# FFN up projections: wide and narrow matmuls taken in turn instead of in runs of 16

## The chip, the cores and the metric

The kernel runs on one core of a Trainium2 chip. The metric is the device time of one execution in microseconds, the median of three runs. TensorE does the matmuls, VectorE and ScalarE the arithmetic around them, GpSimd (POOL) some small things, and SyncE (SP) issues the loads of weights.

## What is computed

A decoder trunk of four layers on 256 tokens of width 1024, in float32. Each layer is half an FFN, a mixer, and half an FFN again, each on a normalised input and added to the residual. The change touches the FFNs alone, of which there are eight:

```python
def swiglu(x, wi, wo):
    gate, up = jnp.split(x @ wi, 2, axis=-1)
    return (jax.nn.silu(gate) * up) @ wo
# for each layer i
h = h + 0.5 * swiglu(rmsnorm(h, ln_ffn1[i]), ffn1_wi[i], ffn1_wo[i])
h = h + mix
h = h + 0.5 * swiglu(rmsnorm(h, ln_ffn2[i]), ffn2_wi[i], ffn2_wo[i])
```

wi has 1024 rows and 2 x 2816 columns, wo has 2816 rows and 1024 columns.

## The kernel before

Float32 products are made of float32r passes. Each operand is split into a high part (rounded) and a low part (the rest), and a product is high x high + high x low + low x high. `whi` and `wlo` hold the two parts of a piece of weights, in a ring of 3 slots; `xT` holds the transposed activations, for each of 8 blocks of 128 rows the high part (256 tokens) and right behind it the low part (256 tokens); `xT_hi` and `xT_lo` are views of it.

The up projection is made transposed: the weights are the stationary operand and the tokens move. So one wide matmul (line 699, `up_both`) with a block of `whi` and all 512 columns of `xT` makes high x high in the left half of a PSUM bank and weight-high x token-low in the right half. One narrow matmul (line 707, `up_rest`) with a block of `wlo` and the 256 columns of `xT_hi` adds the third product to the left half. `psum[:, 4 + blk, :]`, blk 0 to 3, are the four banks: 0 and 1 hold 256 gate columns, 2 and 3 the 256 up columns of a chunk. In the trace an operation is written out<-moving,stationary: `psum<-xT,whi` is the wide and `psum<-xT,wlo` the narrow one.

An FFN has 11 chunks of 256 hidden columns (`FC`). Each takes three pieces of weights: A (rows 0 to 511 of wi, part 0), B (rows 512 to 1023, part 1), C (256 rows of wo, of the chunk before). A part is 4 banks x 4 row blocks k, that is 16 wide and 16 narrow matmuls. Before the change part 0 does its 16 wide ones, then its 16 narrow ones; part 1 the 16 narrow ones, then the 16 wide ones, and after the wide ones of blk 1 it increments `proj_done`, on which ScalarE's gate copy (line 762) waits. The last matmul of each part increments `piece_used`, on which the conversion of the piece after next on ScalarE (lines 474, 478), the up copy (line 766) and by way of them the loads wait. Then come 24 wide matmuls of the down projection (line 536). The waits ahead of blk 0 and 2 of part 0 (`proj_read`) are for the sums on VectorE (lines 815, 821) that read those banks for the chunk before. The order of each engine's work is written out by hand, chunk by chunk; eight chunks of an FFN run in a hardware loop.

The first part 0 of each FFN is in `first_piece`, woven with the transposes of the normalised input. In chunk 0 the matmul of the row scales (line 868) stands after blk 1 of part 1, as `between`.

ScalarE makes `whi` from the loaded `raw`, VectorE then makes `wlo` (line 497). `wlo` of an up piece is not laid out as `whi`: it is moved by `SHIFT` and each row block by a further `STEP`.

```python
SHIFT, STEP = 16, 32
```

Block (k, blk) of `whi` begins at word k x 512 + blk x 128 of its slot, the same block of `wlo` at 16 + k x 544 + blk x 128. Block k of `xT` begins at word k x 512. The `wlo` of other pieces has no shift. The mixer's line 994 (`turned_half`) makes projections with 256 moving columns, weights of `whi` and `wlo` in turn, both without a shift, and moving tokens from `xT`.

Of the kernel before, what the change touches and what calls it, by code (L numbers as in the profile page):

```python
# [27 lines left out]
P = 128  # L28
SEQ = 256
# [8 lines left out]
FC = 256  # L38
CHUNKS = D_FF // FC
RING = 3  # L40
PCOLS = 2048
SHIFT, STEP = 16, 32
# [94 lines left out]
def trunk(nc, x, positions, ln_ffn1, ffn1_wi, ffn1_wo, ln_mix, ln_ffn2, ffn2_wi, ffn2_wo,  # L137
# [3 lines left out]
    with ctx:  # L141
        def sb(name, shape, dt=F32):
            return ctx.enter_context(nc.sbuf_tensor(name, shape, dt))
# [6 lines left out]
        whi = sb("whi", [P, RING, PCOLS], F32R)  # L150
        wlo = sb("wlo", [P, RING, PCOLS + P], F32R)
        h = sb("h", [P, TT, D])
        xT = sb("xT", [P, KD, 2, SEQ], F32R)
        xT_hi, xT_lo = xT[:, :, 0, :], xT[:, :, 1, :]
# [28 lines left out]
        psum = ctx.enter_context(nc.psum_tensor("psum", [P, 8, NCOL], F32))  # L183
# [363 lines left out]
        def out_group(pe, slot, g, xh, xl, k0, first, last):  # L547

            t, nh = GROUPS[g]
            for k in range(2):  # L550
                m = passes(pe, psum[:, g, :], xh[:, k0 + k, t * P:(t + 1) * P], xl[:, k0 + k, t * P:(t + 1) * P],
                           slot, slice(k * D + nh * NCOL, k * D + (nh + 1) * NCOL), first and k == 0, last and k == 1)
            return m
# [27 lines left out]
        def norm_fill0(j):  # L581
            return 0 if j == 0 else subs[j - 1].norm_fill0
# [64 lines left out]
        def first_piece(pe, j):  # L647
# [9 lines left out]
            if s.kind != "ffn" and s.kind != "ml":  # L657
                pe.wait_ge(tr_read, q + 2)
                m = turned_half(pe, s, 0, 0, 0)
                norm_fill(pe, j, 3)  # L660
                m = turned_half(pe, s, 0, 0, 1)
            elif s.kind == "ffn":
                pe.wait_ge(tr_read, q + 2)
                up_both(pe, slot, 0, 0, None if j else lambda k: first_wait(pe, k))
                if j:
                    norm_fill(pe, j, 3)
                up_both(pe, slot, 0, 1)
                up_both(pe, slot, 0, 2)
                up_both(pe, slot, 0, 3)
                for blk in range(4):  # L670
                    m = up_rest(pe, slot, 0, blk)
            else:
                for t in range(TT):
                    if t:
                        norm_fill(pe, j, 3)
                    pe.wait_ge(tr_read, q + t + 1)
                    m = project(pe, slot, t, UP[0][t], 0, p.tiles, p.cols, True, False)
            m.then_inc(piece_used, 1)

        def last_piece(pe, s, n, xh, xl, k0):  # L680

            j = s.index + 1
            pe.wait_ge(lo_ready, n + 1)
            for g in range(4):
                m = out_group(pe, n % RING, g, xh, xl, k0, False, True)
                m.then_inc(acc_done if g < 3 else piece_used, 1)
                if g == 2 and j < len(subs):
                    norm_fill(pe, j, 0)
                    norm_fill(pe, j, 1)
            if j < len(subs):  # L690
                first_piece(pe, j)


        def up_both(pe, slot, part, blk, ready=None):

            for k in range(4):
                if ready:
                    ready(k)
                i = pe.matmul(psum[:, 4 + blk, :], whi[:, slot, k * 2 * FC + blk * P:k * 2 * FC + (blk + 1) * P],  # L699
                              xT[:, 4 * part + k, :, :].rearrange("p a n -> p (a n)"),  # L700
                              start=part == 0 and k == 0, stop=part == 1 and k == 3, skip_group_check=True)
            return i

        def up_rest(pe, slot, part, blk):

            for k in range(4):
                i = pe.matmul(psum[:, 4 + blk, 0:SEQ], wlo[:, slot, SHIFT + k * (2 * FC + STEP) + blk * P:SHIFT + k * (2 * FC + STEP) + (blk + 1) * P],  # L707
                              xT_hi[:, 4 * part + k, :], start=False, stop=False, skip_group_check=True)
            return i

        def ffn_pe(pe, s):
            n0, b0, c0 = s.piece0, s.block0, CHUNKS * s.ffn

            def up(m, c, part, between=None):
                pe.wait_ge(lo_ready, m + 3 * c + 1)
                if part == 0:
                    for blk in range(4):
                        if blk % 2 == 0:
                            pe.wait_ge(proj_read, 2 * b0 - 1 + blk // 2 + 2 * c)
                        up_both(pe, m % RING, 0, blk)  # L720
                    for blk in range(4):
                        i = up_rest(pe, m % RING, 0, blk)
                else:
                    for blk in range(4):
                        up_rest(pe, m % RING, 1, blk)
                    for blk in range(4):
                        i = up_both(pe, m % RING, 1, blk)
                        if blk == 1:
                            i.then_inc(proj_done, 1)
                            if between:  # L730
                                between()
                i.then_inc(piece_used, 1)

            def chunk(c):
                up(n0 - 1, c, 0)
                up(n0, c, 1)
                m = n0 + 1
                pe.wait_ge(lo_ready, m + 3 * c + 1)
                pe.wait_ge(hid_lo_done, c0 + c)
                for g in range(4):  # L740
                    i = out_group(pe, m % RING, g, hidT_hi, hidT_lo, 0, isinstance(c, int) and c == 1, False)
                i.then_inc(piece_used, 1)

            pe.wait_ge(tr_read, norm_fill0(s.index) + 4)
            up(n0 + 1, 0, 1, lambda: rows_pe(pe, s, 0))
            chunk(1)
            with pe.Fori(2, CHUNKS - 1) as c:
                chunk(c)
            chunk(CHUNKS - 1)
            pe.wait_ge(hid_lo_done, c0 + CHUNKS)  # L750
            last_piece(pe, s, n0 + 3 * CHUNKS - 1, xT_hi, xT_lo, 6)
# [114 lines left out]
        def rows_pe(pe, s, bank):  # L866
            pe.wait_ge(diag_done, s.rows0 + 1)
            pe.matmul(psum[:, bank, 0:SEQ], ones[:, :], diag[:, :, :].rearrange("p t n -> p (t n)"), start=True,
                      stop=True).then_inc(rows_done, 1)
# [1388 lines left out]
```

## Time and profile before

| | |
|---|---|
| median of 3 runs | 1925.06 us (1924.36 to 1925.41) |
| the profiled execution | 1924.97 us, span 1923.2 us |
| TensorE busy | 1901.9 us of the span, 99% |
| TensorE, weight loads | 1640.8 us, 85% |
| VectorE | 1366.2 us, 71% |
| ScalarE | 1128.9 us, 59% |
| DMA | 344.41 MB, mean 179 GB/s |

The span is the time from the first to the last instruction in the profile of one execution. Busy time of TensorE includes the modelled ends of the matmuls, which overlap the next ones; so the distance between two starts says more than a duration. A weight load has a row of its own (PEld) and runs beside the matmul ahead of it. "Idle before" is the time for which an engine sat idle ahead of an instruction, and after the arrow stands what released it.

### The profile page before, as it was taken

How to read it: one execution, taken by the hardware profiler on the slowest of the kernel's cores; microseconds unless marked ns; L12 is line 12 of the kernel's file. 1: busy time of each engine (PE TensorE's matmuls, PEld its weight loads, DVE VectorE, ACT ScalarE, POOL GpSimd, SP SyncE). 2: the span in 40 equal slices, each digit the busy share in tenths (PEclk: the TensorE clock that was granted, in tenths of full speed). 3: DMA queues.
4: the chain of work that ended last, by engine and by line, in shares of the span. 5: the costliest groups of instructions: out<-in, count | busy, mean ns of one | idle time of the engine just before them, and what ended most of it. 6: DMA issues, size and time to landing. Idle time of an engine off the chain costs nothing.

```text
span 1923.2 us, 29477 instructions
## 1 busy us (share of the span) xinstructions
PE 1901.9 (99%) x10740; PEld 1640.8 (85%) x10740; DVE 1366.2 (71%) x1844; ACT 1128.9 (59%) x1678; POOL 70.0 (4%) x151
## 2 busy tenths in 40 slices
PE   8999999999999999999999999999999999999998
PEld 6888988888888888888888889888888888978887
DVE  6766775777776687776776676676677777667666
ACT  6555575555655567655565555665555556656553
POOL 2000000000000002000010001000000000000000
PEclk9999999999999999999999999999999999999999
DMA  6555534655555554555655544355556555535553
GB/s 220 197 195 198 175 127 137 218 193 187 167 196 195 177 190 161 170 194 190 211 175 196 196 158 131 126 178 193 196 178 212 191 188 172 175 124 167 191 196 120
DMA packets 245263, 344.41 MB, mean 179 GB/s; under 512 B 12213, under 2 KB 197194, under 8 KB 245194
## 3 DMA queue, kind: packets, MB, share of 16 engines
q1 hardware_dynamic: 242016, 340.29, 53.6%
q10 hardware_dynamic: 3178, 3.18, 0.6%
q8 instruction: 46, 0.75, 0.2%
q14 instruction: 23, 0.19, 0.0%
HBM read 341.32 MB, written 1.06 MB: 178 GB/s over the span
## 4 chain that ended last, share of the span: by engine, by line
PE 93%; DVE 4%; ACT 2%; issue 0%; ACTq 0%; POOL 0%; POOLq 0%; DVEq 0%
PE psum L699 34%; PE psum L536 32%; PE psum L707 17%; PE psum L994 5%; DVE wlo L497 1%; PE psum L567 1%; PE psum L1645 1%; PE psum L1036 1%; DVE mix L1460 1%; ACT whi L478 1%; PE psum L1702 0%; DVE mix L1185 0%; PE psum L1047 0%; PE psum L1732 0%; PE psum L1609 0%
## 5 line engine op out<-in xcount | busy, mean ns | idle before, releaser
L478 ACT ACTIVATE whi<-raw,gains 128x512 fp32r<-128x512 f32 (+2 forms) x876 | 557.0, 709 | 255.1 <-PE psum L707 187.4
L699 PE MATMUL psum<-xT,whi 128*128 128x512 f32 x2816 | 679.2, 392 | 3.0 <-DVE wlo L518 2.5
L497 DVE SCALAR_TENSOR_TENSOR wlo<-raw,gains,whi 128x512 fp32r<-128x512 f32 (+2 forms) x876 | 596.1, 742 | 55.7 <-ACT whi L478 55.7
L699 PEld LDWEIGHTS psum<-xT,whi 128*128 128x128 f32 x2816 | 522.3, 188 | 111.9 <-issue 3.6
L707 PEld LDWEIGHTS psum<-xT,wlo 128*128 128x128 f32 x2816 | 333.2, 188 | 6.8
L707 PE MATMUL psum<-xT,wlo 128*128 128x256 f32 x2816 | 334.7, 276 | 0.0
L815 DVE TENSOR_TENSOR gate_in_T<-psum,low 128x512 f32<-128x512 f32 x88 | 60.9, 692 | 326.0 <-ACT low L762 326.0
L493 DVE TENSOR_TENSOR wlo<-raw,whi 128x2048 fp32r<-128x2048 f32 x100 | 228.6, 2286 | 42.8 <-ACT whi L474 42.8
L536 PE MATMUL psum<-whi,hidT_hi 128*128 128x512 f32 x640 | 249.0, 389 | 0.0
L536 PE MATMUL psum<-wlo,hidT_hi 128*128 128x512 f32 x640 | 249.0, 389 | 0.0
L536 PE MATMUL psum<-whi,hidT_lo 128*128 128x512 f32 x640 | 249.0, 389 | 0.0
L536 PE MATMUL psum<-whi,xT 128*128 128x512 f32 x704 | 229.8, 396 | 2.3 <-DVE xT L562 1.4
L474 ACT ACTIVATE whi<-raw 128x2048 fp32r<-128x2048 f32 x100 | 190.7, 1907 | 26.6 <-PE psum L707 24.5
L536 PEld LDWEIGHTS psum<-whi,xT 128*128 128x128 f32 x704 | 132.2, 188 | 32.7 <-DVE xT L562 3.0
L536 PEld LDWEIGHTS psum<-whi,hidT_hi 128*128 128x128 f32 x640 | 120.1, 188 | 25.0
L536 PEld LDWEIGHTS psum<-wlo,hidT_hi 128*128 128x128 f32 x640 | 120.1, 188 | 24.9
L536 PEld LDWEIGHTS psum<-whi,hidT_lo 128*128 128x128 f32 x640 | 120.1, 188 | 24.9
L536 PE MATMUL psum<-wlo,xT 128*128 128x512 f32 x352 | 137.2, 390 | 0.0
L777 ACT ACTIVATE hidT_hi<-hid 128x512 fp32r<-128x512 f32 x80 | 50.6, 633 | 142.7 <-PE psum L536 106.5
L770 ACT ACTIVATE silu<-gate_in_T 128x512 f32<-128x512 f32 x88 | 55.7, 634 | 106.9 <-DVE gate_in_T L817 106.8
L994 PE MATMUL psum<-xT,whi 128*128 128x256 f32 x576 | 107.1, 285 | 1.1 <-DVE mix L1170 1.1
L762 ACT ACTIVATE low<-psum 128x512 f32<-128x512 f32 x88 | 52.4, 596 | 82.4 <-PE psum L699 82.4
(224 smaller groups left out, 1527.6 us busy)
## 6 DMA issues: line engine op xcount, KB each, us to landing
raw<-in_ffn_wi SPq DMA_DIRECT2D x350, 512.0 KB, 4.6
raw<-in_ffn_wo SPq DMA_DIRECT2D x176, 512.0 KB, 4.4
raw<-in_sb_w_in SPq DMA_DIRECT2D x48, 512.0 KB, 4.6
raw<-in_ml_w_in SPq DMA_DIRECT2D x24, 512.0 KB, 4.6
raw<-in_sb_w_out SPq DMA_DIRECT2D x16, 512.0 KB, 4.0
raw<-in_ml_w_out SPq DMA_DIRECT2D x8, 512.0 KB, 4.0
raw<-in_mla_w_out SPq DMA_DIRECT2D x8, 512.0 KB, 4.2
raw<-in_mla_w_in SPq DMA_DIRECT2D x4, 512.0 KB, 4.2
```

The lines of the kernel that those rows point to most:

```text
L474: act.activation(whi[:, slot, 0:w], raw[:, slot, 0:w], ACT.Copy).then_inc(hi_ready, 1)
L478: last = act.activation(whi[:, slot, r], raw[:, slot, r], ACT.Copy, scale=gain_col(p.gain + k))
L493: dve.tensor_tensor(wlo[:, slot, p.at:p.at + w], raw[:, slot, 0:w], hi[:, 0:w], ALU.subtract).then_inc(lo_ready, 1)
L497: last = dve.scalar_tensor_tensor(wlo[:, slot, p.at + k * p.step + r.start:p.at + k * p.step + r.stop], raw[:, slot, r], gain_col(p.gain + ...
L536: m = pe.matmul(dst, a, b[:, slot, cols], start=first and n == 0, stop=last and n == 2)
L699: i = pe.matmul(psum[:, 4 + blk, :], whi[:, slot, k * 2 * FC + blk * P:k * 2 * FC + (blk + 1) * P], xT[:, 4 * part + k, :, :].rearrange("p ...
L707: i = pe.matmul(psum[:, 4 + blk, 0:SEQ], wlo[:, slot, SHIFT + k * (2 * FC + STEP) + blk * P:SHIFT + k * (2 * FC + STEP) + (blk + 1) * P], ...
L762: act.activation(low[:, 0, :, :], psum[:, 4:6, SEQ:2 * SEQ], ACT.Copy).then_inc(low_done, 1)
L770: act.activation(silu[:, :, :], gate_in_T[:, :, :], ACT.Silu).then_inc(silu_done, 1)
L777: act.activation(hidT(last)[0], hid[:, :, :], ACT.Copy).then_inc(hid_hi_done, 1)
L815: dve.tensor_tensor(gate_in_T[:, :, :], psum[:, 4:6, 0:SEQ], low[:, 0, :, :], ALU.add).then_inc(proj_read, 1)
L994: i = pe.matmul(dst, w[:, m % RING, c:c + P], v[:, k0 + k, :], start=k0 + k == 0 and a == 0 and blk == 0, stop=k0 + k == KD - 1 and a == 2 ...
```

## The change

The two matmuls get functions of their own, `up_wide` and `up_narrow`, and a new `up_mixed` takes them in turn: for each k, in part 0 wide then narrow, in part 1 narrow then wide. `ffn_pe` uses it in both parts. The matmuls, their operands, the waits and the increments are the same; `first_piece` keeps its order. In part 1 `proj_done` is incremented by the last wide matmul of blk 1, as before, which now has 8 narrow and 8 wide ones ahead of and with it instead of 16 narrow and 8 wide.

```diff
+        def up_wide(pe, slot, part, blk, k):
+
+            return pe.matmul(psum[:, 4 + blk, :], whi[:, slot, k * 2 * FC + blk * P:k * 2 * FC + (blk + 1) * P],
+                             xT[:, 4 * part + k, :, :].rearrange("p a n -> p (a n)"),
+                             start=part == 0 and k == 0, stop=part == 1 and k == 3, skip_group_check=True)
+
+        def up_narrow(pe, slot, part, blk, k):
+
+            c = SHIFT + k * (2 * FC + STEP) + blk * P
+            return pe.matmul(psum[:, 4 + blk, 0:SEQ], wlo[:, slot, c:c + P], xT_hi[:, 4 * part + k, :], start=False, stop=False,
+                             skip_group_check=True)
+
...
+        def up_mixed(pe, slot, part, blk):
+
+            for k in range(4):
+                if part == 0:
+                    up_wide(pe, slot, part, blk, k)
+                i = up_narrow(pe, slot, part, blk, k)
+                if part:
+                    i = up_wide(pe, slot, part, blk, k)
             return i
...
                     for blk in range(4):
                         if blk % 2 == 0:
                             pe.wait_ge(proj_read, 2 * b0 - 1 + blk // 2 + 2 * c)
-                        up_both(pe, m % RING, 0, blk)
-                    for blk in range(4):
-                        i = up_rest(pe, m % RING, 0, blk)
+                        i = up_mixed(pe, m % RING, 0, blk)
                 else:
                     for blk in range(4):
-                        up_rest(pe, m % RING, 1, blk)
-                    for blk in range(4):
-                        i = up_both(pe, m % RING, 1, blk)
+                        i = up_mixed(pe, m % RING, 1, blk)
                         if blk == 1:
                             i.then_inc(proj_done, 1)
```

## Rows read from the trace of the kernel before

**Rows 1.** The page: busy time, granted clock, and the chain by line.

```profile
PE 1901.9 (99%) x10740; PEld 1640.8 (85%) x10740; DVE 1366.2 (71%) x1844; ACT 1128.9 (59%) x1678; POOL 70.0 (4%) x151
...
PEclk9999999999999999999999999999999999999999
...
PE psum L699 34%; PE psum L536 32%; PE psum L707 17%; PE psum L994 5%; DVE wlo L497 1%; PE psum L567 1%; PE psum L1645 1%; PE psum L1036 1%; DVE mix L1460 1%; ACT whi L478 1%; PE psum L1702 0%; DVE mix L1185 0%; PE psum L1047 0%; PE psum L1732 0%; PE psum L1609 0%
```

**Rows 2.** Waits of TensorE over the whole span: total us, times, longest.

```profile
PE psum L2219 <- DMA mix<-in_ln_ffn: 6.0, 1, 6.0
PE psum L699 <- DVE wlo L518: 2.5, 2, 1.4
...
PE psum L699 <- DVE gate_in_T L815: 0.4, 1, 0.4
```

**Rows 3.** Timeline of TensorE in one FFN chunk: start us, us, what, count.

```profile
93.10 3.79 PE L699 MATMUL psum<-xT,whi 128*128 128x512 f32 x16
96.73 3.80 PE L707 MATMUL psum<-xT,wlo 128*128 128x256 f32 x32
100.36 3.81 PE L699 MATMUL psum<-xT,whi 128*128 128x512 f32 x16
104.02 0.39 PE L536 MATMUL psum<-whi,hidT_hi 128*128 128x512 f32 x1
```

**Rows 4.** Lines 699, 707: duration ns min/median/max; whole span, then from 100.36 on.

```profile
L699 PE MATMUL psum<-xT,whi x2816: 387/389/795, 10.5 to 1904.0; 128*128 128x512 f32 x188
...
L707 PE MATMUL psum<-xT,wlo x2816: 276/276/388, 19.2 to 1900.5; 128*128 128x256 f32 x188
...
L699 PE MATMUL psum<-xT,whi x1: 395/395/395, 100.4 to 100.4; 128*128 128x512 f32 x1
...
L699 PE MATMUL psum<-xT,whi x2: 395/396/397, 100.4 to 100.6; 128*128 128x512 f32 x2
...
L699 PE MATMUL psum<-xT,whi x2: 389/392/395, 100.8 to 101.1; 128*128 128x512 f32 x2
...
L699 PE MATMUL psum<-xT,whi x8: 389/389/393, 101.3 to 102.9; 128*128 128x512 f32 x8
...
L707 PE MATMUL psum<-xT,wlo x2: 276/277/278, 100.1 to 100.2; 128*128 128x256 f32 x2
```

**Rows 5.** The same: line 707 from 96.73 on, line 699's last before.

```profile
L707 PE MATMUL psum<-xT,wlo x3: 277/279/279, 96.7 to 97.0; 128*128 128x256 f32 x3
...
L707 PE MATMUL psum<-xT,wlo x20: 276/276/276, 97.8 to 99.9; 128*128 128x256 f32 x20
...
L699 PE MATMUL psum<-xT,whi x1: 388/388/388, 96.5 to 96.5; 128*128 128x512 f32 x1
```

**Rows 6.** Lines 994 and 1645, also 256 columns: durations, and part of the timeline.

```profile
L994 PEld LDWEIGHTS psum<-xT,whi x576: 186/192/192, 198.1 to 1672.5; 128*128 128x128 f32 x192
L994 PE MATMUL psum<-xT,whi x576: 278/283/467, 198.1 to 1672.6; 128*128 128x256 f32 x192
...
L1645 PE MATMUL psum<-sp_hi,whi x64: 276/280/416, 1170.0 to 1212.4; 128*128 128x256 f32 x64
...
198.70 0.28 PE L994 MATMUL psum<-xT,wlo 128*128 128x256 f32 x1
...
199.06 0.28 PE L994 MATMUL psum<-xT,wlo 128*128 128x256 f32 x1
```

**Rows 7.** Timeline of ScalarE and VectorE in the chunk of rows 3.

```profile
102.40 0.60 ACT L762 ACTIVATE low<-psum 128x512 f32<-128x512 f32 x1 [1.03 <-PE psum L699]
...
104.37 2.73 DVE L497 SCALAR_TENSOR_TENSOR wlo<-raw,gains,whi 128x512 fp32r<-128x512 f32 x4
```

**Rows 8.** Timeline at the first chunk: the diag tile on POOL, the row matmul.

```profile
19.71 1.21 POOL L2144 TENSOR_SCALAR diag<-ident,rstd 128x128 f32<-128x128 f32 x2
...
25.16 0.59 PE L868 MATMUL psum<-diag,ones 128*128 128x256 f32 x2
```

More of the change, by code:

```diff
@@ L698, in up_both @@
                     ready(k)
-                i = pe.matmul(psum[:, 4 + blk, :], whi[:, slot, k * 2 * FC + blk * P:k * 2 * FC + (blk + 1) * P],
-                              xT[:, 4 * part + k, :, :].rearrange("p a n -> p (a n)"),
-                              start=part == 0 and k == 0, stop=part == 1 and k == 3, skip_group_check=True)
+                i = up_wide(pe, slot, part, blk, k)
             return i
@@ L706, in up_rest @@
             for k in range(4):
-                i = pe.matmul(psum[:, 4 + blk, 0:SEQ], wlo[:, slot, SHIFT + k * (2 * FC + STEP) + blk * P:SHIFT + k * (2 * FC + STEP) + (blk + 1) * P],
-                              xT_hi[:, 4 * part + k, :], start=False, stop=False, skip_group_check=True)
+                i = up_narrow(pe, slot, part, blk, k)
+            return i
+        def up_mixed(pe, slot, part, blk):
+            for k in range(4):
+                if part == 0:
+                    up_wide(pe, slot, part, blk, k)
+                i = up_narrow(pe, slot, part, blk, k)
+                if part:
+                    i = up_wide(pe, slot, part, blk, k)
             return i
```

## The prediction

> **What bounds the kernel now.** I read the page first: TensorE is busy 99% of the span, and the chain that ended last lies for 34% on the wide up matmuls (line 699), 17% on the narrow ones (line 707) and 32% on the down projections and outputs (line 536) [rows 1]. TensorE's granted clock is in the top tenth in all 40 slices, so at the upper level of 2.4 GHz [rows 1]. Then the waits of TensorE: seven kinds, the longest 6.0 us in all, once, before the first matmul; the others are 2.5 us or less, down to 0.4 [rows 2]. So there is next to no wait to remove; the time is the number of matmuls times the distance from one start to the next, which I call the pitch. The timeline of one FFN chunk gives the pitches, by the difference of the starts of two groups divided by the count [rows 3]: 16 wide ones from 93.10 to 96.73, 3.63/16 = 0.227 us; 32 narrow ones (16 of each part) to 100.36, 3.63/32 = 0.1134 us; 16 wide ones to 104.02, 3.66/16 = 0.2288 us. Both widths cost the same 0.443 ns per column, with the weight load of each matmul hidden behind the matmul ahead of it. The third stretch is the same work as the first and takes 0.03 us longer. It is the one that follows narrow matmuls, and this is the row on which the forecast turns.
>
> The duration in a row is modelled and longer than the pitch, but it moves with it: 389 ns stands for a pitch of 227 and 276 for 113.4 [rows 3, 4], and 283 for 120 [rows 6], each 162 to 163 more. So differences of durations can be used as differences of pitch.
>
> **The change part by part.** Nothing is added or taken away: the same 2816 wide and 2816 narrow matmuls [rows 4], with the same operands, waits and increments. The first piece of each of the 8 FFNs keeps its old order (16 of each). That leaves 2816 - 8 x 16 = 2688 pairs whose order becomes wide, narrow, wide, narrow (in part 1 narrow first).
>
> Part A, the cost of a switch of width. Of a wide matmul after a narrow one the trace has an example in every chunk, 88 in all. The rows around 100.36 us show the first five wide durations as 395, 397, 389, 395, 393 and then 389 on and on [rows 4]: in the second row 397 is the new one beside 395, in the third 389 and 395, in the fourth 393 is the largest. The excess is 6 + 8 + 0 + 6 + 4 = 24 ns, which is the 0.03 us seen above. I read it as two regular reads (the moving columns and the next weights) that settle into a phase, and that a change of width unsettles. Of a narrow one after a wide one: 279, 279, 277, then 276 [rows 5], an excess of 3 + 3 + 1 = 7 ns, 80 of which would go (the 8 first pieces keep theirs). After the change every matmul of the 2688 pairs is the first after a switch, and none gets to settle. For the wide one I take +6, the value of a first one; its bounds are 387 - 389 = -2, the least wide duration at this line, and 397 - 389 = +8 [rows 4]. Sum: 2688 x 6 ns = 16.1 us.
>
> Part B, the narrow one. By its place it is a first one, +3. But what is loaded behind it changes too. Today the weights loaded during a narrow matmul are nearly always narrow ones (wlo, laid out at SHIFT and STEP, 16 + k x 544 + blk x 128 words); after the change they are wide ones (whi, at k x 512 + blk x 128, no shift). Line 994 is the nearest row with that: matmuls of the same width and type, with weights of whi and wlo both unshifted, and there the duration is 283, the weight load lasts 192 instead of 188, and three matmuls take 0.36 us, a pitch of 120 instead of 113.4 [rows 6]. That is +7. The one narrow matmul of a chunk that today loads whi behind it showed 278, +2 [rows 4], and line 1645, of the same width with whi as weights but another moving tile, has 276 at least and 280 as its median [rows 6], so the 7 isn't certain. Bounds: 0 (the 276) and +7. I take +5, midway between 3 and 7. Sum: 2688 x 5 = 13.4 us.
>
> The opposite of this could be true of the wide one: it would now load the shifted wlo behind it. The one wide matmul of a chunk that does so today lasted 388, against 389 [rows 5], so I count nothing for it, and keep it as a rival.
>
> Part C, what is removed. The switches of today vanish into the pairs: 88 x 24 ns + 80 x 7 ns = 2.1 + 0.6 = 2.7 us.
>
> The Trainium skill speaks of this on the page "TensorE: Matmul & The Clock Gate", section "What happens when you issue a matmul": weights and moving data have read ports of their own, so loading the next weights takes nothing from the running matmul. By that rule a pair costs the same in any order, and the result would be no change beyond part C, which is the time of the first rival below. The row of line 994 speaks against it: equal width, equal type, another address of the weights, and 6.6 ns more.
>
> Part D, the waits. The increment on the wide matmul of blk 1 in part 1 comes earlier: today after 16 narrow and 8 wide, then after 8 pairs, (16 x 113.4 + 8 x 227) - 8 x 340.4 = 0.9 us earlier. ScalarE sits in that wait for the gate copy (1.03 us ahead of 102.40), then VectorE waits for ScalarE; the copy, the gate sum and the conversion queued behind it on VectorE move 0.9 us ahead [rows 7]. That buys nothing: the conversion from 104.37 to 107.10 is wanted by TensorE after the 24 matmuls that start at 104.02 [rows 3], at 104.02 + 24 x 0.2267 = 109.46, so it is early already by 2.4 us. In part 0 the wait ahead of blk 2, for the up sum, is reached after 8 pairs in place of 8 wide ones, 0.9 us later: more slack; that ahead of blk 0 stays. At most the 0.4 us wait for the gate sum [rows 2] goes. The up copy still waits for the last matmul of part 1, whose place is the same. The increments on which the conversions and so the loads hang are on the last matmul of each part, as now, and no DMA or queue is moved. The small matmul of the row scales (line 868) comes 0.9 us earlier in the first chunk; its input is the diag tile, done at 19.71 + 1.21 = 20.92 with the matmul at 25.16, so of 4.2 us of cover 3.3 remain [rows 8]. I count D at zero. If that cover were gone, each us by which a conversion came too late would be a us more; it has 2.4 in hand, and a slower part gives it more.
>
> Sum: 16.1 + 13.4 - 2.7 = +26.8 us. The profiled execution took 1924.97 us, 0.1 below the median of 1925.06, with a span of 1923.2. Forecast: 1924.97 + 26.8 = 1951.8 us, +1.4%. By the bounds of this case, 6 + 3 = 9 and 8 + 7 = 15 ns per pair, 1946.5 to 1962.6.
>
> **The rivals.** First: the alternation settles into a phase of its own. Runs of one width do that within five matmuls, and a strict alternation is regular too. A settled pair costs 340 ns, nothing but part C is left, and the time is 1922.3. For it: how sharply both runs lock. Against: the narrow run and the wide run clearly don't share a phase, or the switch would cost nothing. With -2 on the wide one it would be 1916.9.
>
> Second, faster: the shifted layout helps whatever matmul it is loaded behind. It saves the narrow ones 120 - 113.4 = 6.6 ns; if wide ones gain as much once wlo is loaded behind them, and narrow ones keep their 113.4 with whi behind them (as the 278 half suggests), a pair falls by 6.6 and the time is 1924.97 - 17.7 - 2.7 = 1904.6. It decides if wide durations come out near 382. Against: the 388 of the one that does it today, and that nothing wide at line 699 lies below 387.
>
> Third, much slower: each pair pays the whole of both disturbances, 24 + 7 = 31 ns. That gives 2688 x 31 = 83.3, and 2005.6. Against: most of the 24 falls on later matmuls, which the next switch cuts off.
>
> **How the numbers follow.** Forecast 0.62. Settled alternation 0.15, of which 0.13 within 0.2% and 0.02 at its fast end. The layout gain 0.12. The whole price 0.06. A tax of a few ns per pair, between 1929 and 1946, 0.05. A measurement of this kernel can tell about 0.2%, 3.9 us. So slower 0.62 + 0.06 + 0.05 = 0.73, same 0.13, faster 0.14. The range from 1917 to 1963 takes in the forecast, the settled case and the small tax, 0.82; the forecast's own is 1946.5 to 1962.6.
>
> **What would show it.** In the profile after: the median of line 699 near 395 and of line 707 near 281; a chunk's up part of 16 pairs at 5.6 us instead of 5.44; line 536 still 389; the waits of TensorE no longer than now; line 762 starting 0.9 us earlier in its part. Medians of 389 and 276 mean the first rival, 382 the second. The forecast is wrong if the unsettled state isn't what a switch costs but what a long run of the other width leaves behind: then a single narrow matmul would disturb nothing.

## The result and the profile after

| | median | runs |
|---|---|---|
| before | 1924.71 us | 4 (1924.24 to 1925.41) |
| changed | 1950.22 us | 4 (1948.98 to 1951.53) |
| ratio | 1.0131 | 95% interval 1.0115 to 1.0147 |

The change costs 25.5 us, 1.3%. The forecast was 1951.8 us. The profiled execution took 1951.53 us with a span of 1949.8 us, 26.6 more than the 1923.2 of before.

The page of the changed kernel first: busy time of the engines, the chain by line, and the groups of the wide (now line 696) and the narrow matmul (now line 703), with busy us and mean ns.

```profile
PE 1927.1 (99%) x10732; PEld 1655.2 (85%) x10740; DVE 1371.6 (70%) x1844; ACT 1135.5 (58%) x1678; POOL 70.0 (4%) x151
...
PE psum L696 34%; PE psum L536 31%; PE psum L703 17%; PE psum L1009 5%; DVE wlo L497 2%; PE psum L1660 1%; PE psum L567 1%; ACT whi L478 1%; PE psum L1051 1%; DVE mix L1475 1%; PE psum L1717 0%; DVE mix L1200 0%; DMA raw<-in_ffn_wi 0%; DMA raw<-in_ml_w_in 0%; PE psum L1062 0%
...
L696 PE MATMUL psum<-xT,whi 128*128 128x512 f32 x2816 | 987.1, 397 | 1.5 <-DVE wlo L518 1.5
L703 PE MATMUL psum<-xT,wlo 128*128 128x256 f32 x2816 | 756.9, 281 | 0.0
```

The two groups invite a mistake. Together their busy time is 1744 us, while that of the same groups before, on the same page, was 1013.9 (679.2 and 334.7). That is not what the change costs: the busy time of a group merges its own matmuls where their modelled ends overlap. In a run a wide matmul adds its pitch of 227 ns to that sum. In alternation the next wide one starts some 351 ns later, so it adds 351, the narrow one's share included, and a narrow one adds its whole 281. TensorE as a whole went from 1901.9 to 1927.1, 25.2 us; the other 1.4 us of the span are time in which it sat idle. The means are of more use: 397 and 281.

The timeline of one chunk, with the start of each matmul in us:

```profile
77.53 0.39 PE L696 MATMUL psum<-xT,whi 128*128 128x512 f32 x1
77.75 0.28 PE L703 MATMUL psum<-xT,wlo 128*128 128x256 f32 x1
77.87 0.40 PE L696 MATMUL psum<-xT,whi 128*128 128x512 f32 x1
78.11 0.28 PE L703 MATMUL psum<-xT,wlo 128*128 128x256 f32 x1
78.22 0.39 PE L696 MATMUL psum<-xT,whi 128*128 128x512 f32 x1
78.45 0.28 PE L703 MATMUL psum<-xT,wlo 128*128 128x256 f32 x1
78.57 0.40 PE L696 MATMUL psum<-xT,whi 128*128 128x512 f32 x1
78.81 0.28 PE L703 MATMUL psum<-xT,wlo 128*128 128x256 f32 x1
78.92 0.39 PE L696 MATMUL psum<-xT,whi 128*128 128x512 f32 x1
...
88.77 0.39 PE L536 MATMUL psum<-whi,hidT_hi 128*128 128x512 f32 x1
```

This answers [rows 3]. From the first up matmul to the first down matmul it is 88.77 - 77.53 = 11.24 us, against 104.02 - 93.10 = 10.92 before; at the trace's ns it is 11240 and 10913, the same to 1 ns in each of the 72 chunks that stand between two down projections. The pattern repeats after two pairs: from 77.87 to 78.57 and from 78.22 to 78.92 are 0.70 us, so 350 ns a pair. The wide pitches are 229.3 and 235.9 in turn, the narrow ones 117.2 and 117.6. Part 1 takes five pairs to settle and is then in another cycle, with wide pitches of 235 to 236 and narrow ones of 117 to 118, 353 ns a pair, though wide and narrow take turns there with the same places of their weights. By part the chunk costs 5598 ns (5446 before) and 5642 ns (5467 before).

Durations of the two lines and of a down group (ns, min/median/max), against [rows 4]:

```profile
L696 PE MATMUL psum<-xT,whi x2816: 387/397/796, 10.9 to 1930.6; 128*128 128x512 f32 x188
...
L703 PE MATMUL psum<-xT,wlo x2816: 276/281/468, 19.2 to 1930.5; 128*128 128x256 f32 x188
...
L536 PE MATMUL psum<-whi,hidT_hi x640: 389/389/389, 38.7 to 1935.6; 128*128 128x512 f32 x160
```

The wide median went from 389 to 397, the narrow one from 276 to 281; the down projections stayed at 389. 327 ns x 72 steady chunks are 23.5 us of the 26.6. Part 1 of the first chunk and the whole second chunk of each FFN are in the new order too, but together they add only 1.1 us over the eight FFNs, because something is won there. The gate sum on VectorE that the second chunk's first matmul waits for, in one FFN before and after:

```profile
324.53 0.69 DVE L815 TENSOR_TENSOR gate_in_T<-psum,low 128x512 f32<-128x512 f32 x1 [2.69 <-ACT low L762]
...
326.77 0.69 DVE L830 TENSOR_TENSOR gate_in_T<-psum,low 128x512 f32<-128x512 f32 x1 [1.84 <-ACT low L777]
```

Before, the sum ends at 325.22, and the matmul that waits for it starts at 325.37, 396 ns behind the one ahead of it instead of 227; the next one is late by another 78. That is a stop of 0.25 us in seven FFNs and of 0.61 in one, 2.3 us in all. After the change the increment of `proj_done` comes earlier, the sum ends at 327.46, the matmul starts at 328.42, and no such distance is left. The remaining 2.0 us lie between the FFNs' chunks. 1.6 of them are one wait in a mixer (line 1645, now 1660), 0.8 us before and 2.4 after; it doesn't go with the order, since it is 0.8 in e2, which alternates too, and 2.4 in e7, which has runs.

The gate copy in the chunk of the timeline and the waits of TensorE:

```profile
86.15 0.60 ACT L777 ACTIVATE low<-psum 128x512 f32<-128x512 f32 x1 [0.19 <-PE psum L696]
```

```profile
PE psum L2234 <- DMA mix<-in_ln_ffn: 5.1, 1, 5.1
PE psum L1660 <- DVE mix L1946: 2.4, 1, 2.4
PE psum L696 <- DVE wlo L518: 1.5, 2, 1.1
PE psum L536 <- DVE xT L562: 1.4, 3, 0.6
```

The copy starts 86.15 - 83.13 = 3.02 us into part 1, against 102.40 - 98.55 = 3.85 before, so 0.83 us earlier. TensorE's waits came to 13.1 us before and 14.3 after: 1.6 more in the mixer, the 0.4 for the gate sum gone, small differences elsewhere. Of the stops at the gate sum this view showed only that 0.4, since the others are shorter than the modelled end of the matmul ahead. In the steady chunks nothing was won or lost by waits.

### The profile page after: what moved, and what is told of

The parts are those of the page before. It is cut to its first block, busy times and chain, and to the rows that moved or that the text cites. A ratio compares the mean times of both kernels' runs of the same rounds, so it can differ in the third digit from the quotient of the medians.

```text
span 1949.8 us, 29469 instructions
## 1 busy us (share of the span) xinstructions
PE 1927.1 (99%) x10732; PEld 1655.2 (85%) x10740; DVE 1371.6 (70%) x1844; ACT 1135.5 (58%) x1678; POOL 70.0 (4%) x151
## 4 chain that ended last, share of the span: by engine, by line
PE 93%; DVE 4%; ACT 2%; DMA 1%; issue 0%; SPq 0%; ACTq 0%; POOL 0%; POOLq 0%
PE psum L696 34%; PE psum L536 31%; PE psum L703 17%; PE psum L1009 5%; DVE wlo L497 2%; PE psum L1660 1%; PE psum L567 1%; ACT whi L478 1%; PE psum L1051 1%; DVE mix L1475 1%; PE psum L1717 0%; DVE mix L1200 0%; DMA raw<-in_ffn_wi 0%; DMA raw<-in_ml_w_in 0%; PE psum L1062 0%
## 5 line engine op out<-in xcount | busy, mean ns | idle before, releaser
L696 PE MATMUL psum<-xT,whi 128*128 128x512 f32 x2816 | 987.1, 397 | 1.5 <-DVE wlo L518 1.5
L703 PE MATMUL psum<-xT,wlo 128*128 128x256 f32 x2816 | 756.9, 281 | 0.0
L696 PEld LDWEIGHTS psum<-xT,whi 128*128 128x128 f32 x2816 | 529.8, 189 | 123.8 <-DVE wlo L518 2.3
L703 PEld LDWEIGHTS psum<-xT,wlo 128*128 128x128 f32 x2816 | 521.5, 188 | 7.8
L1009 PEld LDWEIGHTS psum<-xT,whi 128*128 128x128 f32 x576 | 90.7, 192 | 1.9 <-DVE mix L1185 1.5
```

Of the source, the lines that this page charges most:

```text
L696: return pe.matmul(psum[:, 4 + blk, :], whi[:, slot, k * 2 * FC + blk * P:k * 2 * FC + (blk + 1) * P], xT[:, 4 * part + k, :, :].rearrange ...
L703: return pe.matmul(psum[:, 4 + blk, 0:SEQ], wlo[:, slot, c:c + P], xT_hi[:, 4 * part + k, :], start=False, stop=False, skip_group_check=True)
L1009: i = pe.matmul(dst, w[:, m % RING, c:c + P], v[:, k0 + k, :], start=k0 + k == 0 and a == 0 and blk == 0, stop=k0 + k == KD - 1 and a == 2 ...
```

## The experiments

The pitches below are differences of starts. "Runs" is the order of before, "alternation" that of the change. Where a time has no interval it is one execution, beside one of before on the same chip (1924.3 to 1925.6 us throughout).

My theory going in: a matmul is disturbed when what happens beside it changes from one matmul to the next, above all the width. The rival: what counts is where the weights lie that are loaded behind it. These four came first.

**e1, the address alone.** Runs, with

```diff
-SHIFT, STEP = 16, 32
+SHIFT, STEP = 0, 0
```

> The kernel before (runs of 16) with SHIFT and STEP at 0, so that wlo lies as whi does. It prices the address alone, with no alternation. If the layout is what keeps a narrow matmul at a pitch of 113.4 ns, the narrow ones go to 120 ns as line 994 shows (duration 283 in place of 276), and 2816 x 6.6 ns = 18.6 us come on top: about 1943 us. If the width alone sets the pitch, nothing moves: 1925 us. The wide ones stay at 227 in either case.

Measured 1943.52 us against 1925.05, +18.5. The timeline of a chunk, and the durations of line 707:

```profile
77.38 3.79 PE L699 MATMUL psum<-xT,whi 128*128 128x512 f32 x16
81.01 4.00 PE L707 MATMUL psum<-xT,wlo 128*128 128x256 f32 x32
84.84 3.82 PE L699 MATMUL psum<-xT,whi 128*128 128x512 f32 x16
88.50 0.39 PE L536 MATMUL psum<-whi,hidT_hi 128*128 128x512 f32 x1
...
L707 PE MATMUL psum<-xT,wlo x2816: 277/283/385, 19.1 to 1919.1; 128*128 128x256 f32 x188
```

32 narrow matmuls take 84.84 - 81.01 = 3.83 us, 120 ns each, where it was 113.4; the wide runs are unchanged. Same matmuls, same order, same waits, only wlo lies 16 words and a step elsewhere: 6.6 ns each. The page "TensorE: Matmul & The Clock Gate" of the Trainium skill has it that loading the next weights takes nothing from the running matmul ("What happens when you issue a matmul"); here the pitch depends on the address of the weights, so the measurement decides.

**e2, alternation without the shift.** The same diff on the changed kernel.

> The changed kernel (alternation) with SHIFT and STEP at 0. Theory (a switch of width unsettles the reads, wherever wlo lies): the wide ones stay between 229 and 238 ns, the narrow ones near 117 to 120, and the time within 8 us of the changed kernel's 1950. Rival (the address of the weights loaded behind the wide matmul counts, and the shift helps there): the wide ones take some 6.6 ns more, 2688 x 6.6 = 17.7 us, so 1968 us.

Measured 1954.57 us, +4.4 on the changed kernel. The cycle is now three pairs long: wide 232.5, 240.8, 235.8, narrow 113.3, 117.5, 120.0, in sum 1060 ns, so 353.3 a pair. A chunk is 53 ns longer than in the changed kernel, 4.2 us over 80. The theory's number held and the rival's 1968 didn't come. Taking the shift away costs 18.5 us in runs and 4.4 in alternation: the layout had been fitted to the runs.

**e3, runs of 4.** `up_mixed` does the four wide ones of a bank, then the four narrow ones (the other way round in part 1).

> Bank by bank: 4 wide then 4 narrow in part 0, 4 narrow then 4 wide in part 1. If the tax is paid at each switch of width and decays over the next matmuls as in the kernel before, a run of 4 wide ones pays 6 + 9 + 2 + 6 = 23 ns by starts and a run of 4 narrow ones 8; 7 of each per chunk make 217 ns, less the 34 of the kernel before, so +183 ns x 80 chunks = +15 us: about 1940 us, with the wide ones at 232.5, 235.8, 228.4, 232.5 and the narrow ones at 117.5, 116, 114, 113. If the tax doesn't depend on the length of a run: 1950 us. If only the alternation of single matmuls costs: 1925 us.

Measured 1935.45 us. The pitches are those forecast but for the last of each wide four: 232.5, 235.8, 228.3, 229.2 and 117.5, 115.8, 114.2, 113.3; a chunk's up part is 11.07 us. I had 232.5 for the fourth, which is 1.8 us of the 4.6 by which the time lies below the 1940 expected; the stop at the gate sum, 2.3 us, isn't there in this order either. So the disturbance at a switch is real and fades over several matmuls.

**e5, all up matmuls 512 wide, in alternation.** The extra columns are weight-low x token-low, a term that the other kernels leave out.

```diff
-            return pe.matmul(psum[:, 4 + blk, 0:SEQ], wlo[:, slot, c:c + P], xT_hi[:, 4 * part + k, :], start=False, stop=False,
+            return pe.matmul(psum[:, 4 + blk, :], wlo[:, slot, c:c + P],
+                             xT[:, 4 * part + k, :, :].rearrange("p a n -> p (a n)"), start=False, stop=False,
```

> The changed kernel with the narrow matmul made 512 columns wide (it also adds weight-low x token-low to the right half, a term that the kernel leaves out otherwise). whi and wlo still alternate, with their addresses; only the switch of width is gone. Theory (width): all 64 up matmuls of a chunk settle at 227 ns, a chunk's up part is 64 x 226.7 = 14.51 us, and the time 1925 - 3 + 2816 x 0.1133 = 2241 us. Rival (the alternation of whi and wlo or their addresses cost, not the width): pitches of 230 to 236 stay, 5 to 9 ns on 5376 matmuls, so 2268 to 2290 us.

Measured 2263.84 us, 23 above the theory and 4 below the rival. The widths are equal and still nothing settles at 227:

```profile
L696 PE MATMUL psum<-xT,whi x2816: 387/392/797, 10.6 to 2242.9; 128*128 128x512 f32 x188
...
L703 PE MATMUL psum<-xT,wlo x2816: 387/394/581, 18.5 to 2242.7; 128*128 128x512 f32 x188
```

Medians of 392 and 394, pitches of 225.8 to 235.9, 14.77 us for a chunk's 64. So the switch of width isn't needed. The theory in its first form had fallen: the switch from whi to wlo, which lie differently, disturbs too.

The next four go after the addresses, and e4 after the parts.

**e8, the same with SHIFT and STEP at 0.**

> All up matmuls 512 wide and in alternation, with SHIFT and STEP at 0: whi and wlo now lie alike and the widths are alike, so that nothing changes from one matmul to the next. Theory (what costs is a change from one matmul to the next, of width or of the weights' place on the 128-word grid): the pitch settles at 227 ns, an up part pair of 64 matmuls takes 14.51 us, and the time is about 2241 us against the 2263.8 of the same kernel with the shift. Rival (going back and forth between the two tiles costs by itself): it stays near 2264.

Measured 2237.94 us, 25.9 below e5.

```profile
L696 PE MATMUL psum<-xT,whi x2816: 387/389/796, 10.8 to 2217.0; 128*128 128x512 f32 x188
...
L703 PE MATMUL psum<-xT,wlo x2816: 387/389/577, 18.2 to 2216.8; 128*128 128x512 f32 x188
```

Both medians are 389, every one of the 64 pitches in a steady chunk is 226.7, and the chunk takes 14.51 us. Two tiles in strict alternation, and not a ns lost: with equal widths it was the layout alone.

**e4, alternation in part 0 alone.** Part 1 of the changed kernel goes back to 16 narrow, then 16 wide.

> Alternation in part 0 alone; part 1 back to 16 narrow, then 16 wide. It checks that the cost adds up by part. From the trace of the changed kernel part 0 costs 350.0 ns a pair (229.4 and 235.9 for the wide ones in turn, 117.2 and 117.6 for the narrow) against 340.0, so 16 x 10 ns less the 8 ns switch that goes, +152 ns x 80 chunks = +12 us: 1937 us. If what part 0 leaves behind disturbs part 1's first run further, more; if the two parts don't add up, the rest up to 1950 comes from neither alone.

Measured 1944.70 us, 8 above the expectation: a miss. Part 0 takes its 5598 ns as forecast. The rest is in part 1. Its narrow run, which in the kernel before sits at 113.4 with the same tiles and addresses, starts behind part 0's last narrow matmul:

```profile
82.79 2.20 PE L703 MATMUL psum<-xT,wlo 128*128 128x256 f32 x17
...
L703 PE MATMUL psum<-xT,wlo x14: 282/283/283, 83.0 to 84.6; 128*128 128x256 f32 x14
```

The run's duration is 283 in place of 276; the pitches alternate between 121.7 and 118.3, 120.0 on average, and never come down. The 16 narrow ones take 105 ns more and the wide ones behind them 16 less, so part 1 has 5556 ns in place of 5467: 89 ns x 80 = 7.1 us of the miss of 7.7. So the same run has two states in which it stays, and what ran ahead of it decides which. The parts don't simply add up.

**e6 and e7, whi moved by 16 words** against the grid of 128 words on which xT lies, for every use of whi, in alternation and in runs. Of the tiles of the up and down matmuls whi alone moves; the tiles allocated behind `y`, which the mixers use, move by 16 words with it.

```diff
-        whi = sb("whi", [P, RING, PCOLS], F32R)
...
         y = sb("y", [P, TT, D])
+        pad = sb("pad", [P, 16])
+        whi = sb("whi", [P, RING, PCOLS], F32R)
```

> The changed kernel with whi allocated 16 words off the 128-word grid on which xT lies, so that the wide weights too are shifted against the moving columns. Theory (the tax comes from the relation of the addresses of the two reads as it changes from matmul to matmul): the cycle of pitches changes, and with both weights off the grid the narrow ones, which load whi behind them, come to 113 to 117 and the pair to 340 to 348 ns: 1925 to 1945 us. Rival (the switch of width is what costs, whatever the address): the pair stays within 2 ns of 351.7 and the time near 1950. The down projections move whi as their columns, so their 227 may change too; this is read by line 536.

> The kernel before with the same move of whi by 16 words. If the wide matmul gains from shifted weights as the narrow one does (6.6 ns), its runs go from 227 to 220 ns and the time falls by some 2816 x 6.6 = 18.6 us to 1906; then a layout beats both kernels. If a wide matmul has room behind it for its weight load at any address, it stays at 227 and the time at 1925 within 3 us, with the down projections as they are.

e6 took 1951.64 us. The up pair fell to 347 ns as the theory had it (229.2 and 118.3, 229.2 and 116.7; chunk 11.10 us instead of 11.24, 10.9 us in all), but the time didn't, since the down projections, which move whi as columns, rose from 389 to medians of 397, 391 and 397 in their three groups of 640: (8 + 2 + 8) x 640 = 11.5 us. By starts 24 of them take 5.59 us instead of 5.44, a pitch of 232.9 for 226.7. There the moving tile was moved and the stationary one, hidT, was not, so the place of the moving columns counts too.

e7 took 1956.75 us, and neither expectation had allowed for that: the shift that helps the narrow one hurts the wide one. Its chunk, and a down group (line 537):

```profile
77.89 3.89 PE L700 MATMUL psum<-xT,whi 128*128 128x512 f32 x16
81.63 3.84 PE L708 MATMUL psum<-xT,wlo 128*128 128x256 f32 x32
85.31 3.89 PE L700 MATMUL psum<-xT,whi 128*128 128x512 f32 x16
89.03 0.39 PE L537 MATMUL psum<-whi,hidT_hi 128*128 128x512 f32 x1
...
L537 PE MATMUL psum<-whi,hidT_hi x640: 388/397/398, 38.9 to 1940.7; 128*128 128x512 f32 x160
L537 PE MATMUL psum<-wlo,hidT_hi x640: 390/392/401, 39.1 to 1940.9; 128*128 128x512 f32 x160
```

16 wide ones take 81.63 - 77.89 = 3.74 us, 233.3 each, and the down group's median is 397.

**e9, the grid.** None of the model is computed: TensorE alone runs the two matmuls on fixed tiles, in sections of 24 or of 24 pairs, with the weights at `off + k * 512 + blk * 128` and the columns on the grid.

```python
def wide(n, off, step=0):
    blk, k = n // 4 % 4, n % 4
    c = off + k * (512 + step) + blk * P
    return pe.matmul(psum[:, 4 + blk, :], whi[:, c:c + P], xT[:, k, :, :].rearrange("p a n -> p (a n)"), ...)
```

> None of the model: only matmuls of the two forms on fixed tiles, in sections of 24 (one width) or 24 pairs (alternation), with the stationary weights moved off the 128-word grid of the moving columns by 0, 16, ... 112 words, 8 + 8 sections of one width, 64 of the two in alternation, and three with the shift and step of the kernel. It prices the disputed cost by itself, without other engines. Theory (the pitch hangs on where each weight read falls against the moving read, and on what changes from one matmul to the next): wide at 0 settles at 227 ns and at 16 near 233; narrow at 0 at 120; alternation at (0, 0) near 353 ns a pair and with the kernel's shift near 350; the pairs differ among the 64 by 10 ns or more. Rival (other engines' traffic in the real kernel makes the differences): every wide section is at 227, every narrow one at 113, and every pair at 340 here. If one of the 64 pairs is at 340 or below, the alternation could be had for nothing with another layout; if none is, the order costs at any address.

Settled pitch in ns, from the starts of the last 8 of a run and of the last 12 pairs. All values but five repeat after 64 words (off 64 as off 0, and so on, within 0.2 ns), so a quarter of the grid is enough:

```
one width        off 0     16     32     48
  wide           226.6  233.4  232.4  229.3
  narrow         120.0  113.4  119.0  117.9

a pair           narrow 0     16     32     48
  wide 0            346.7  346.7  346.7  350.0
  wide 16           350.0  353.3  350.0  353.3
  wide 32           352.2  346.7  351.2  346.7
  wide 48           340.0  346.7  353.3  353.3
```

(The exceptions: the cell 0, 0 has 346.7 here and 353.3 in its three repeats, as in e2 and in e11's section of the same cell; and wide 16 with narrow 0 has 350.0, but 353.3 where narrow is at 64. Such a cell has more than one state, as the run in e4 has.) Two cells in the durations of lines 61 (wide) and 67 (narrow): first wide 0, narrow 0 from 91.3 to 95.3 us, then wide 48, narrow 0 from 303.4 to 307.3 us:

```profile
L61 PE MATMUL psum<-xT,whi x13: 391/391/391, 91.0 to 95.2; 128*128 128x512 f32 x13
...
L67 PE MATMUL psum<-xT,wlo x12: 280/280/280, 91.3 to 95.1; 128*128 128x256 f32 x12
...
L61 PE MATMUL psum<-xT,whi x13: 389/389/389, 303.1 to 307.2; 128*128 128x512 f32 x13
...
L67 PE MATMUL psum<-xT,wlo x12: 276/276/276, 303.4 to 307.1; 128*128 128x256 f32 x12
```

391 and 280 against 389 and 276, the same two values that a wide and a narrow run settle at. And the narrow run twice, first at off 16 without a step, then with the kernel's own shift and step:

```profile
L67 PE MATMUL psum<-xT,wlo x14: 276/276/276, 65.4 to 66.9; 128*128 128x256 f32 x14
...
L67 PE MATMUL psum<-xT,wlo x19: 282/283/283, 670.7 to 672.9; 128*128 128x256 f32 x19
```

With the kernel's layout it sits at 283 here, where it is entered from the four 128-column matmuls that divide the sections, and at 276 in the kernel before, where it is entered from a wide run. These are the two states of e4. With that layout for wlo the alternation came to 117, 229, 118, 236 ns here, the very cycle of the changed kernel, with no other engine at work. So other engines' traffic has no part in that cycle.

**e10, alternation with the layout of that cell.** Up pieces only:

```diff
-SHIFT, STEP = 16, 32
+SHIFT = 48
...
-            return pe.matmul(psum[:, 4 + blk, :], whi[:, slot, k * 2 * FC + blk * P:k * 2 * FC + (blk + 1) * P],
+            return pe.matmul(psum[:, 4 + blk, :], whi[:, slot, SHIFT + k * 2 * FC + blk * P:SHIFT + k * 2 * FC + (blk + 1) * P],
...
-            c = SHIFT + k * (2 * FC + STEP) + blk * P
+            c = k * 2 * FC + blk * P
```

and the conversions write whi at the shift and wlo without.

> The changed kernel with another layout: the whi of an up piece is moved by 48 words in its slot, its wlo by none (SHIFT off wlo, no STEP); the order of the matmuls is that of the changed kernel. In the grid of bare matmuls this cell (48, 0) settled at 340.0 ns a pair, the sum of 227 and 113.3. Theory (the tax of the alternation is a matter of the addresses alone): a chunk's up part falls from 11.24 to some 10.88 to 10.91 us, and the time to 1922 to 1926 us, the 27 us of the change given back. Rival (in the kernel the pair comes from 24 down matmuls and from one part into the next, and settles in another cycle): 346 to 353 ns a pair and 1938 to 1955 us.

Measured 1922.51 us (10 runs, 1921.09 to 1924.23) against 1924.67 (13 runs), ratio 0.9988, interval 0.9979 to 0.9998. The start of a chunk, a stretch of its part 0, and its first down matmul:

```profile
75.75 0.40 PE L696 MATMUL psum<-xT,whi 128*128 128x512 f32 x1
75.99 0.28 PE L703 MATMUL psum<-xT,wlo 128*128 128x256 f32 x1
...
78.49 0.39 PE L696 MATMUL psum<-xT,whi 128*128 128x512 f32 x1
78.71 0.28 PE L703 MATMUL psum<-xT,wlo 128*128 128x256 f32 x1
78.83 0.39 PE L696 MATMUL psum<-xT,whi 128*128 128x512 f32 x1
79.05 0.28 PE L703 MATMUL psum<-xT,wlo 128*128 128x256 f32 x1
79.17 0.39 PE L696 MATMUL psum<-xT,whi 128*128 128x512 f32 x1
...
86.66 0.39 PE L536 MATMUL psum<-whi,hidT_hi 128*128 128x512 f32 x1
```

The first pair costs more (235.8 and 117.5; in part 1 121.7 and 231.7), and from the third on each costs 340.0: from 78.49 to 79.17 two pairs, 0.68 us. The up part is 86.66 - 75.75 = 10.91 us. The order of the change, with the same matmuls and waits, costs nothing here. The chunk is 6 ns shorter than in the kernel before, 0.5 us in all. Of the other 1.2 us by which the span is shorter (1921.5 against 1923.2), 1.0 lies at the start, ahead of the first down matmul. The heads of the later FFNs are shorter by some 0.2 us each, as the stop at the gate sum is gone here too, and against that the wait in the mixer is 2.4 us, as in the changed kernel, and not 0.8.

**e12, runs on that layout.**

> The order of the kernel before (runs of 16) on the layout of the last trial (whi of an up piece moved by 48 words, wlo by none). It completes the square of two orders and two layouts. Theory (order and layout have to match): in the grid of bare matmuls wide ones at 48 settled at 229.25 ns and narrow ones at 0 at 120.0, so a chunk's up part takes about 32 x 229.25 + 32 x 120 = 11.18 us against 10.91, and the time is 1925 + 80 x 0.265 = about 1946 us, give or take 3 for what the switches add. Rival (the layout is better for any order): 1925 us or less.

Measured 1943.85 us against 1925.57.

```profile
76.32 3.83 PE L696 MATMUL psum<-xT,whi 128*128 128x512 f32 x16
79.99 3.98 PE L703 MATMUL psum<-xT,wlo 128*128 128x256 f32 x32
83.81 3.82 PE L696 MATMUL psum<-xT,whi 128*128 128x512 f32 x16
87.47 0.39 PE L536 MATMUL psum<-whi,hidT_hi 128*128 128x512 f32 x1
```

The narrow ones take 3.82 us, 119.4 each, and the wide ones 3.67 and 3.66, 229 each. That completes the square:

| | wlo shifted (16, step 32) | whi shifted (48) |
|---|---|---|
| runs of 16 | 1924.7 us | 1943.9 us |
| alternation | 1950.2 us | 1922.5 us |

**e11, the fine grid.** As e9, in steps of 4 words from 0 to 60, 256 cells of 20 pairs.

> None of the model: the grid again in steps of 4 words from 0 to 60 (the grid before repeated itself after 64 words): 16 sections of each width and 256 of the alternation, 20 pairs each. If the floor of a pair is the sum of the two settled runs, no cell is below 340 ns and no run of one width below 226.6 or 113.3. If the 16-word steps hid a better place, some cell is at 333 or less, and the order of the change could win there.

No cell is below 340.0. Three are at it: (16, 4), (48, 0) and (48, 4). The mean is 349.4 and the highest 355.6; 346.7, 350.0 and 353.3 are the common ones. Wide runs settle at 226.7 at 36 words and between 228.3 and 234.2 elsewhere (the one at 0 was the first work of the kernel, with pitches of 427 ns at its head, and isn't used; e9's section at 64 stands for it, 226.8); narrow ones at 113.3 at 16 words alone, and between 116.7 and 120.0 elsewhere. So 227 + 113.3 is the least that a pair came to on this grid. Each cell was entered in one way only, and the cell 0, 0 shows that another entry can lead to another value, so it isn't shown that no layout goes lower. Well-laid runs are at these values too, and an alternation at 340.0 can only save what their switches cost, 34 ns a chunk; in e10 its own first pairs cost 28 of them.

## Why the prediction held, and what in it did not

- *What bounds the kernel.* Held: in the steady chunks there is no wait, only the pitch, and all of the change there is in it.
- *Part A, the wide one at +6.* Right in sign, somewhat small: 232.6 on average in part 0 (+5.9), some 235 in part 1, +7 over the chunk. The cause given for it was wrong. "None gets to settle" isn't so: the alternation settles, in part 0 at once, in a cycle of two pairs that costs 10 ns a pair over 340, and in part 1 within five pairs, at 13 ns a pair. That its mean is near the first value after a switch, 232.5, is luck. e8 and e10 show it: strict alternation of two tiles at 227, and strict alternation of two widths at 340 a pair, for nothing.
- *Part B, the narrow one at +5.* +4 over the chunk (117.2 to 118.5). The surplus of 1 here makes up for what part A lacked, which is luck again. The step itself, that the unshifted whi behind it is what would cost up to 7, has e1 for it where all weights are alike (+6.6), but in alternation the two addresses can't be priced one by one: narrow 0 has 340.0 with wide 48 and 346.7 to 353.3 with the others.
- *Part C.* The switches of a chunk were worth 24 + 7 = 31 ns by durations and 34 by starts, so 32 x 11 - 31 = 321 ns a chunk was the forecast, and 327 was measured.
- *Part D.* The increment came 0.83 us earlier, for 0.9, and in the steady chunks that had no effect. But it was not zero: "at most the 0.4 us wait for the gate sum" was too little, since each FFN had a stop there that the view of the waits didn't show, and 2.3 us went.
- *The sum.* +26.8 was forecast; +26.6 by the spans and +25.5 by the medians was measured. The pitches alone came to 27.0; the stops took 2.3 off and the waits between the chunks, a mixer's above all, put 2.0 on. That these two cancel is luck as well.
- *First rival, a settled alternation at 340 (0.15).* Half right: it does settle. What was missing is that the settled value depends on the layout; with another one it is 340, and e10 measured 1922.5 us beside the rival's 1922.3. That number agrees in part by chance: a chunk of e10 is 6 ns below the kernel before and not the 34 of part C, and the rest is the start and the waits.
- *Second rival, the shift helps what it is loaded behind (0.12).* Fell: the wide durations went to 397, not to 382, and e7 shows that a shift of 16 costs a wide run 6.6 ns instead of saving it.
- *Third rival, the whole price at each pair.* Fell: 11.3 ns a pair ((327 + 34)/32), not 31.
- *What would show it wrong.* That "a single narrow matmul would disturb nothing" came true in e10, at another layout.

So the number was right for a reason that was only half so: the trace of before showed that a switch costs a few ns each time and that the address mattered, but I put the cost of alternation down to the width and to never settling. What was shown: in alternation the settled pitch depends on the weights' addresses modulo 64 words, on the order and on the state that was entered, the cycle is the same with no other engine at work, and in e5 and e8, with equal widths, the layout made the whole difference. That two reads of one memory collide is my picture of it and only argued: no row shows the memory. The moving tile was shifted only in the down projections of e6 and e7, where the pitch rose too, and never on a grid of its own, so it is open whether the distance between the two addresses counts or each by itself.

## What to carry to other kernels

Where TensorE has no waits, subtract the starts of neighbouring matmuls: a pitch some ns above the settled one, thousands of times, is the whole of a 1% change, and neither busy shares nor waits show it. The same subtraction finds stops that are shorter than the modelled end of a matmul and so stand in no list of waits, like the 0.25 us at the gate sum. A layout of the weights that was fitted to one order of matmuls is part of that order: change one and the other has to be searched again, and a small kernel of bare matmuls finds the place in one run. Price an edit of the order by its own settled cycle, in the state in which it is entered, not by the first values after a switch in another pattern.

## What the runs showed of the hardware

- In float32r, at a granted clock of 0.996 to 1.000, the pitch of a 512-column matmul in the settled cycles of these kernels ranges from 225.8 to 241 ns and that of a 256-column one from 113.3 to 121.7, by the place of the tiles, the order and the state entered. Runs of one width were at 226.6 and 113.3 on average at best. In e9 59 of 64 pairs of places repeat after 64 words (256 bytes) per partition, and the other five are cells with more than one state.
- The place of the moving columns counts too: with whi, as the columns of the down projections, moved by 16 words the pitch rose from 226.7 to 232.9 (e6).
- Settled states of an alternation come in cycles of one pair (e10), two (part 0 of the changed kernel) or three (e2), in the fine grid of more as well (five pairs at wide 24, narrow 36), and are exact: the 72 steady chunks of a kernel agree within 1 ns in 11 us.
- The same narrow run has two states, 113.3 and 120 ns, and keeps the one it is entered in for 32 matmuls (the kernel before) and 16 (e4), as long as the runs were. The alternation of the changed kernel has two as well, 350 ns a pair in part 0 and 353 in part 1.
